# Eight of eleven gated-pair combinations built during the up rounds, and the norm work reordered at group changes

## The chip, the cores and the metric

The kernel runs on one core of a Trainium2 chip. The metric is the device time of one execution in microseconds (us), here the median of repeated runs. The engines are TensorE (PE in the profile; PEld is its weight load), VectorE (DVE), ScalarE (ACT), GpSimd (POOL) and SyncE (SP), which here only starts DMA transfers.

## What is computed

One layer of a streaming encoder on 2048 prompt and 64 sample tokens with 1024 channels. The change touches the second half of the layer, a gated feed-forward network, and the final norm:

```
h = modulate(x, norm_ffn_g, shift, scale)
up, cf_new = causal_dwconv(h @ ffn_up_w, cf_prev, ffn_conv_w, ffn_conv_b)   # 1024 -> 2 * 2816, width 3
val, gt = split(up, 2)
x = x + gate * ((val * gelu(gt)) @ ffn_down_w)                              # 2816 -> 1024
y = rmsnorm(x, final_norm_g)
```

## The kernel before

The 2112 tokens lie along the free dimension in two halves of 1056, the channels on the 128 partitions. Every matrix is held as float32 and multiplied as a pair of float16 numbers, high and low, in three passes (high by high, high by low, low by high). Large products use one level of a seven-product scheme over 2 by 2 blocks, so each operand needs seven combinations of its four blocks: some are the blocks, the others sums made of them. A combination costs the sums (GpSimd), a float16 copy of it (ScalarE, "hi") and the rest as float16 (VectorE, "lo").

**Up rounds.** 22 rounds, one for each pair of 128-row tiles (value and gate), each of 7 products times 3 token pieces `q` of 352 columns times 12 matmuls = 252 matmuls of 352 columns (`block_product`, `passes`, L2886). ScalarE copies products out of PSUM (`copy` L1658, `c21` L1666) and computes the first tap of the convolution (`first_tap` L1695) and the gelu; VectorE adds products (`block` L2547, L2550, L2553), computes two taps (`ffn_conv` L2563, L2567), multiplies value by gate (`product` L2571) and splits the next round's weights (`up_lo` L2495). SP stores the gated product of the round (the hidden tile) to DRAM as `ffn_hidden` (`store_hidden`). Beside this, 44 "units" (combinations of the down weights, `unit_*`) are made two a round, three in rounds 17 to 20, and stored to DRAM as `down_combinations`.

**Down phase.** Hidden tiles go in 11 pairs `i` (two tiles of 128 rows each). The tokens go in 3 groups `g` of 352 columns in each half, and the output rows in 4 pairs of 128-row tiles, so there are 12 steps `n = 4 g + (0..3)`; `pair_of` turns the order round in every second group, so that the weights need no reload at a group change. A step is 7 products of 11 pairs of 3 matmuls, 231 matmuls of 352 columns (`down_product`, L3131), cut into chunks of pairs (`chunks_of`) so that weights of the next step can be loaded into `dwt` as soon as a chunk is through. `dact` has 11 slots, one for each pair, with the seven combinations of one group. In every group all 11 slots are filled from `ffn_hidden`: a load into one of two staging buffers (`base_load`, L937), four sums on GpSimd (`base_sums`, L1146 to L1151), two copies on ScalarE (`base_hi`, L1727, L1729), two subtractions on VectorE (`base_lo`, L2584, L2586):

```
dve.wait_ge(b_hi, 2 * s + 1)
dve.tensor_tensor(dact[i][:, 0:3, 1], stage_of(s)[:, 1:4], dact[i][:, 0:3, 0], ALU.subtract)
dve.wait_ge(b_hi, 2 * s + 2)
dve.tensor_tensor(dact[i][:, 3:7, 1], dsum[s % 2], dact[i][:, 3:7, 0], ALU.subtract)
```

A slot may be overwritten when the last step of the group has used it, and in group 0 when the up phase's `hTc` under it is free. The queues are written out by hand, in program order for each engine. At a group change (n = 3 and 7) ScalarE and VectorE have `base_hi`/`base_lo` of five pairs ahead of the first evacuation of step n, another in the middle, and the others after it. The evacuation of a step is `first_copy` (ScalarE L1849), `fourth_copy`, and on VectorE `top_left` to `bottom_left` with the residual update `y_update` (L2679); it is followed by squares (`square2`) and their sum over tiles (`add_square`, L2731, L2733). After four steps TensorE sums over partitions by a float32 matmul with ones (`sum_squares2`, L3095), placed between products of the next group's first chunk, ScalarE takes the root (`root2`, L1868), VectorE the reciprocal (`inverse`, L2737) and the scaling (`finish`, L2740), and SP stores y (L967, `store_y`) and loads the next residual (L961).

## Time and profile before

| what | value |
|---|---|
| median of 3 runs | 2797.05 us (2796.39 to 2802.14) |
| profiled execution, its own time | 2797.01 us |
| its span in the profile | 2794.9 us |
| TensorE busy | 2674.5 us, 96% |
| VectorE, ScalarE, GpSimd busy | 1761.8, 1367.9, 580.9 us |
| up rounds | 1433.8 to 2264.0 us of the span |
| down phase, to TensorE's last matmul | 2264.0 to 2783.8 us |

The span is the profiled part of the execution; 2.1 us of its time lie outside. Busy shares are averages over stages with different limits, and PE counts as busy at half clock too.

### The profile page before, as it was taken

To read this page: it belongs to the slowest core of one execution; us is meant where nothing else is said; L and a number is where in the kernel's file an instruction comes from. 1 tells how busy PE (TensorE), PEld (TensorE's weight loads), DVE (VectorE), ACT (ScalarE), POOL (GpSimd) and SP (SyncE) were. 2 spreads that over 40 slices of the span, in tenths; PEclk is the share of its full clock that TensorE was granted. 3 is DMA by queue.
4 is the path that set the end of the run, shared out by engine and by line. 5 is a ranking of instruction groups with operands and counts; after the bars stand their busy time and mean duration, and the time that the engine had idled before them with its cause. 6 is when DMAs were issued, how large, how long until landed. Compare 5 with 4: busy or idle time off the path is not lost. (4 is left out here: it accounts for less than half of the span.)

```text
span 2794.9 us, 50241 instructions
## 1 busy us (share of the span) xinstructions
PE 2674.5 (96%) x18662; PEld 1786.5 (64%) x18662; DVE 1761.8 (63%) x3321; ACT 1367.9 (49%) x2618; POOL 580.9 (21%) x603
## 2 busy tenths in 40 slices
PE   7999999999999999999999999999999988879797
PEld 2466666666678886559986666666666655546464
DVE  4966464646466665777787766667777773462723
ACT  4966574747466662125565444544445542232311
POOL 2600000000047894000001010111101162431600
PEclk9999999999999999999999999999999999989898
DMA  8722122220554442656532222222222354464452
GB/s 275 209 89 101 63 69 99 75 102 24 163 162 114 121 185 93 223 189 162 152 93 97 98 81 101 84 101 97 102 99 101 128 210 173 144 210 153 131 216 88
DMA packets 206280, 361.76 MB, mean 129 GB/s; under 512 B 56784, under 2 KB 144848, under 8 KB 200992
## 3 DMA queue, kind: packets, MB, share of 16 engines
q1 hardware_dynamic: 196192, 348.10, 37.8%
q10 hardware_dynamic: 8848, 8.74, 0.9%
q8 instruction: 109, 1.79, 0.3%
q0 software_dynamic: 1072, 2.65, 0.3%
q14 instruction: 59, 0.48, 0.1%
HBM read 252.42 MB, written 109.64 MB: 130 GB/s over the span
## 5 line engine op out<-in xcount | busy, mean ns | idle before, releaser
L2886 PE MATMUL ps<-arena 128*128 128x352 f16 (+1 forms) x11880 | 1611.4, 297 | 4.6 <-DVE arena L2495 1.7
L2886 PEld LDWEIGHTS ps<-arena 128*128 128x128 f16 x11880 | 1101.3, 97 | 510.2 <-DVE arena L2062 2.3
L3131 PE MATMUL ps<-arena 128*128 128x352 f16 x2772 | 438.9, 322 | 43.8 <-DVE arena L2586 26.7
L3131 PEld LDWEIGHTS ps<-arena 128*128 128x128 f16 x2772 | 275.8, 100 | 207.5 <-DVE arena L2586 21.9
L1120 POOL TENSOR_TENSOR arena<-arena 128x128 f32<-128x128 f32 x44 | 22.8, 519 | 1038.9 <-DMA arena<-in_w_down 1038.9
L1658 ACT ACTIVATE arena<-ps 128x352 f32<-128x352 f32 x264 | 119.3, 463 | 201.2 <-PE ps L2886 201.2
L2495 DVE SCALAR_TENSOR_TENSOR arena<-arena 128x512 f16<-128x512 f32 x154 | 104.5, 692 | 142.0 <-ACT arena L1621 142.0
L2992 PE MATMUL ps<-arena 128*128 128x424 f16 (+1 forms) x960 | 173.6, 342 | 1.9 <-DVE arena L2374 1.3
L2978 PE MATMUL ps<-arena 128*128 128x64 f32 (+2 forms) x1200 | 152.2, 273 | 0.5 <-DVE arena L2338 0.5
L2978 PEld LDWEIGHTS ps<-arena 128*128 128x128 f32 (+2 forms) x1200 | 146.0, 194 | 3.3 <-issue 1.8
L1076 POOL CAST arena<-arena 64x512 f16<-64x512 f32 x8 | 4.9, 608 | 688.2 <-DMA arena<-in_cache_kT 688.0
L2992 PEld LDWEIGHTS ps<-arena 128*128 128x128 f16 x960 | 92.5, 97 | 82.6 <-issue 2.3
L1297 ACT ACTIVATE arena<-ps 128x352 f32<-128x352 f32 x192 | 80.8, 462 | 121.4 <-PE ps L2886 121.4
L1695 ACT ACTIVATE arena<-arena 128x2114 f32<-128x2114 f32 x44 | 94.5, 2148 | 69.9 <-DVE arena L2550 69.7
L2563 DVE SCALAR_TENSOR_TENSOR arena<-arena 128x2114 f32<-128x2114 f32 x44 | 106.4, 2417 | 34.0 <-ACT arena L1695 34.0
L1506 ACT ACTIVATE arena<-ps 128x512 f32<-128x512 f32 (+3 forms) x136 | 76.2, 561 | 104.8 <-PE ps L2965 104.7
L1104 POOL TENSOR_TENSOR arena<-arena 128x1024 f32<-128x1024 f32 (+6 forms) x147 | 119.1, 810 | 13.8 <-POOL arena L1097 3.9
L2062 DVE SCALAR_TENSOR_TENSOR arena<-arena 128x512 f16<-128x512 f32 x112 | 73.8, 686 | 64.9 <-ACT arena L1276 64.7
L2567 DVE SCALAR_TENSOR_TENSOR arena<-arena 128x2114 f32<-128x2114 f32 x44 | 107.9, 2452 | 0.4
L1499 ACT ACTIVATE arena<-arena 128x640 f32<-128x640 f32 (+5 forms) x136 | 102.7, 755 | 4.7 <-DVE arena L2317 4.5
L2687 DVE TENSOR_TENSOR arena<-ps,arena 128x352 f32<-128x352 f32 x12 | 6.3, 523 | 151.8 <-PE ps L3131 150.5
L2317 DVE CUSTOM_DVE_ANT_0 arena<-ps,arena 128x640 f32<-128x640 f32 (+5 forms) x136 | 100.2, 737 | 0.3 <-issue 0.2
(234 smaller groups left out, 3418.8 us busy)
## 6 DMA issues: line engine op xcount, KB each, us to landing
arena<-ffn_hidden SPq DMA_DIRECT2D x33, 704.0 KB, 4.1
arena<-in_w_up SPq DMA_DIRECT2D x44, 512.0 KB, 3.9
down_combinations<-arena SPq DMA_DIRECT2D x44, 448.0 KB, 2.7
arena<-down_combinations SPq DMA_DIRECT2D x10, 1792.0 KB, 7.1
arena<-down_combinations SPq DMA_DIRECT2D x20, 896.0 KB, 6.3
arena<-gates SPq DMA_DIRECT2D x8, 2112.0 KB, 9.5
arena<-in_w_proj SPq DMA_DIRECT2D x32, 512.0 KB, 4.4
gates<-arena SPq DMA_DIRECT2D x16, 1024.0 KB, 7.6
```

The lines of the kernel that those rows point to most:

```text
L1104: pool.tensor_tensor(out, djunk[:, :, 0:w], djunk[:, :, w:2 * w], ALU.add).then_inc(ada_step, 1)
L1499: act.activation(pr[0:x.rows, x.h, 0:x.w], pr[0:x.rows, x.h, 0:x.w], ACT.Exp, scale=-1.0, bias=least[0:x.rows, x.h:x.h + 1], accum_out=sm[ ...
L1658: act.activation(fcp[(0, 1, 2, 0)[i]][q], ps[:, bank_of((0, 2, 3, 4)[i], q), 0:CF], ACT.Copy, scale=CSF)\
L1695: act.activation(out, u[:, 0:LF], ACT.Identity, scale=w0, bias=fb).then_inc(f_tap, 1)
L2317: dve.tensor_tensor_reduce(pr[0:rows, h, 0:w], src, bias[x.b][0:rows, h, x.b0:x.b0 + w], 1.0, 3.0e38, ALU.add, ALU.min, least[0:rows, h:h ...
L2495: dve.scalar_tensor_tensor(fsp[:, c, :, 1, :], src.rearrange("p (k m) -> p k m", k=4), -WSF if c == 6 else WSF, fsp[:, c, :, 0, :], ALU.mu ...
L2563: dve.scalar_tensor_tensor(out, u[:, 1:1 + LF], tap(1), out, ALU.mult, ALU.add).then_inc(f_conv, 1)
L2567: dve.scalar_tensor_tensor(out, u[:, 2:2 + LF], tap(2), out, ALU.mult, ALU.add).then_inc(f_conv, 1)
L2886: mm = pe.matmul(out, wt[:, k, wp, :], act_t[:, k, hp], start=(first and k == 0 and n == 0), stop=(last and k == K - 1 and n == 2), skip_g ...
L2978: mm = pe.matmul(ps[0:x.rows, 6, 64 * x.h:64 * x.h + 64], pt[0:k, x.h, c * P:c * P + x.rows], vv[x.b][0:k, x.v0 + c, 64 * x.h:64 * x.h + 6 ...
L2992: mm = pe.matmul(out, wt[:, wp, k, :], mixT[:, k, hp, t:t + w], start=(k == k0 and m == 0), stop=(k == k1 - 1 and m == 2))
L3131: mm = pe.matmul(ps[:, down_bank(n, k), 0:CF], dwt(i)[:, wi, wp, :], dact[i][:, bi, hp, :], start=(i == 0 and m == 0), stop=(i == NI - 1 a ...
```

## The change

- Of the 11 pairs, the first 8 (`NQ`) have their combinations made during up rounds 3 to 18, as 48 "items": one item is one pair in one of six pieces of 176 columns in each half (`HW`). An item is a load of 704 columns from `ffn_hidden`, four sums of 176 columns (`four_sums`), two copies (`item_hi`), two subtractions (`item_lo`), and a store of 4928 bytes a partition to the new DRAM tensor `hidden_combinations`. There are three items and two units in each of these 16 rounds, three units in rounds 1, 2, 19 and 20. Items have one input buffer (`itemr`), one for sums (`isum`), and one for the result (`iout`).
- In the down phase the slots 0 to 7 are filled by one DMA each (`slot_load`). Pairs 8 to 10 (`NB` = 3) go on as before, now as halves of 2 by 176 columns.
- A combination that was a sum by itself now replaces a block in the buffer (`four_sums`, `unit_sums`), so that four combinations are split with the blocks and three with the sums, and `FACTORS` follows.
- The last step of a group goes in seven chunks, single pairs at first; step 10 ends in single pairs.
- At a group change the order on ScalarE and VectorE is the whole evacuation of the step, then a pair, a root or reciprocal, a pair, the other root or reciprocal, a pair. The reciprocal goes to a buffer of its own (`grs`); scaling and store of the third and fourth tile pairs move behind the evacuation of the next two steps. `sum_squares2` stands one product later.

```diff
+NB = 3
+NQ = NI - NB
+HW = CF // 2
...
+        itemr = at_(46914, 4 * HW).rearrange("p (b t) -> p b t", b=4)
+        isum = at_(47618, 3 * HW).rearrange("p (b t) -> p b t", b=3)
+        iout = at_(52000, 7 * 2 * HW, F16).rearrange("p (c s t) -> p c s t", c=7, s=2)
...
-        dact = [at_(3584 + 7 * CF * i, 7 * 2 * CF, F16).rearrange("p (c s t) -> p c s t", c=7, s=2) for i in range(NI)]
+        dact = [at_(3584 + 7 * CF * i, 7 * 2 * CF, F16).rearrange("p (w c s t) -> p w c s t", w=2, c=7, s=2) for i in range(NI)]
...
+            if n == ND - 1:
+                return [(0, NI)]
+            if n % 4 == 3:
+                return [(i, i + 1) for i in range(4)] + [(4, 6), (6, NQ), (NQ, NI)]
+            if n == ND - 2:
+                return [(0, 4), (4, NQ)] + [(i, i + 1) for i in range(NQ, NI)]
+            return [(0, 4), (4, NQ), (NQ, NI)]
...
-        FACTORS = ((0, 0), (1, 2), (4, 5), (3, 3), (5, 4), (6, 1), (2, 6))
+        FACTORS = ((1, 1), (2, 3), (5, 5), (4, 4), (0, 0), (6, 2), (3, 6))
...
+        def units_of(f):
+            return [3 * f - 3 + u for u in range(3)] if f < 3 else [3 * f - 19 + u for u in range(3)]
+        def loop_units(i, late):
+            return [4 * i + 6 + 2 * late + u for u in range(2)]
+        def loop_items(i, late):
+            return [(6 * i + 3 * late + u, (3 * late + u) // 2, (3 * late + u) % 2) for u in range(3)]
...
+            def item_load(n, i, q):
+                sp.wait_ge(b_lo, 2 * n + 2)
+                sp.wait_ge(h_stored, 192 * i + 192)
+                sp.dma_start(itemr.rearrange("p b t -> p (b t)"),
+                             hid_d[:, q, ds(2 * i, 2)].rearrange("p k h t -> p (k h t)")).then_inc(b_loaded[0], 16)
+            def item_store(n, i, q):
+                sp.wait_ge(b_lo, 2 * n + 4)
+                sp.dma_start(hdc_d[:, q // 2, ds(i, 1), q % 2].rearrange("p a c s t -> p (a c s t)"),
+                             iout.rearrange("p c s t -> p (c s t)")).then_inc(item_stored, 16)
...
+            def loop_transfers(i, late):
+                f = round_a(i) + late
+                (n0, _, _), (n1, _, _), (n2, _, _) = loop_items(i, late)
+                u0, u1 = loop_units(i, late)
+                q = 3 * late
+                up_tiles(f + 1)
+                item_store(n0, i, q)
+                item_load(n1, i, q + 1)
+                store_hidden(f - 1)
+                item_store(n1, i, q + 1)
+                item_load(n2, i, q + 2)
+                unit_store(u0)
+                unit_load(u1)
+                item_store(n2, i, q + 2)
+                if late:
+                    item_load(n2 + 1, i + 1, 0)
+                else:
+                    item_load(n2 + 1, i, 3)
+                unit_store(u1)
+                unit_load(u1 + 1)
...
+            def slot_load(g, i):
+                sp.dma_start(dact[i].rearrange("p w c s t -> p (w c s t)"),
+                             hdc_d[:, g, i].rearrange("p w c s t -> p (w c s t)")).then_inc(a_loaded[i // 4], 16)
...
+            first_slots(0, 1)
             store_hidden(LAST - 1)
-            base_load(2)
-            base_load(3)
-            base_load(4)
-            sp.wait_ge(p_filled, up_done(LAST, 3, 2))
+            first_slots(1, 3)
+            first_slots(3, 5)
             weight_load(0, 1, 0)
-            base_load(5)
+            first_slots(5, 7)
+            first_slots(7, 8)
             sp.wait_ge(p_filled, up_done(LAST, 6, 2))
             weight_load(0, 1, 1)
             sp.wait_ge(f_ev, 6 + 6 * NF)
             sp.wait_ge(f_c22, 3 * NF)
             weight_load(0, 2, 0)
             weight_load(0, 2, 1)
-            base_load(6)
-            base_load(7)
             store_hidden(LAST)
             weight_load(0, 2, 2)
+            base_load(2)
...
+                if i == 3:
+                    for k in range(NQ):
+                        sp.wait_ge(q_filled, pair_used(n, k))
+                        slot_load(g + 1, k)
+                    base_load(NB * (g + 1) + 2)
                     store_y(g, 0)
+                    continue
+                if i == 2 and g < NG - 1:
+                    base_load(NB * (g + 1))
+                    base_load(NB * (g + 1) + 1)
+                if n:
+                    next_weights(n, 0)
+                if g and i == 0:
+                    next_residual(g - 1, 0)
+                    store_y(g - 1, 1)
+                if g and i == 1:
+                    store_y(g - 1, 3)
+                next_weights(n, 1)
+                if g and i == 0:
+                    next_residual(g - 1, 1)
+                if g and i == 1:
+                    next_residual(g - 1, 3)
+                next_weights(n, 2)
+                if g and i == 0:
+                    store_y(g - 1, 2)
+                    next_residual(g - 1, 2)
...
+            def four_sums(blocks, sums, at0):
+                b12, b11, b22, b21 = blocks
+                t0, t2, t3 = sums
+                pool.tensor_tensor(t0, b12, b11, ALU.subtract).then_inc(b_sum, 1)
+                pool.wait_ge(b_sum, at0 + 1)
+                pool.tensor_tensor(b12, b22, b12, ALU.subtract).then_inc(b_sum, 1)
+                pool.tensor_tensor(t2, b22, t0, ALU.subtract).then_inc(b_sum, 1)
+                pool.wait_ge(b_sum, at0 + 3)
+                pool.tensor_tensor(t3, b21, t2, ALU.subtract).then_inc(b_sum, 1)
...
+            def loop_sums(i, late):
+                (n0, _, _), (n1, _, _), (n2, _, _) = loop_items(i, late)
+                u0, u1 = loop_units(i, late)
+                item_sums(n0)
+                item_sums(n1)
+                unit_sums(u0)
+                item_sums(n2)
+                unit_sums(u1)
...
+            def item_hi(n):
+                act.wait_ge(item_stored, ITEM_BASE + 16 * n)
+                act.wait_ge(b_sum, 4 * n + 4)
+                act.activation(iout[:, 0:4, 0], itemr, ACT.Copy).then_inc(b_hi, 1)
+                act.activation(iout[:, 4:7, 0], isum, ACT.Copy).then_inc(b_hi, 1)
...
-            def ffn_round(f, late=False):
-                units = [] if tile_is(f, LAST) else wu_units(f, late)
+            def ffn_round(f, units, items=()):
                 if not tile_is(f, 1):
                     for q in range(3):
                         c21(f - 1, q)
...
                     act.wait_ge(p_filled, up_done(f - 1, c, 2))
                     up_hi(f, c)
                 first_tap(f - 1, 1)
+                if items:
+                    item_hi(items[0][0])
                 for q in range(3):
                     copy(f, 0, q)
                 gelu(f - 1, 0)
                 gelu(f - 1, 1)
                 pads(f)
                 copy(f, 1, 0)
+                if items:
+                    item_hi(items[1][0])
...
             for n in range(ND):
-                g, last = n // 4, n % 4 == 3 and n < ND - 1
-                s = NI * (g + 1)
-                if last:
-                    for k in range(5):
-                        base_hi(s + k)
+                g, s = n // 4, NB * (n // 4 + 1)
                 first_copy(n)
-                if last:
-                    base_hi(s + 5)
                 fourth_copy(n)
                 for k in range(4):
                     square2(n, k)
                     if n == ND - 1 and k == 2:
                         root2(g, 0)
-                if last:
-                    base_hi(s + 6)
-                    base_hi(s + 7)
-                    for h in range(2):
-                        root2(g, h)
-                    for k in range(8, NI):
-                        base_hi(s + k)
+                if n % 4 == 3 and n < ND - 1:
+                    base_hi(s)
+                    root2(g, 0)
+                    base_hi(s + 1)
+                    root2(g, 1)
+                    base_hi(s + 2)
             root2(NG - 1, 1)
...
+            def item_lo(n):
+                dve.wait_ge(b_hi, 2 * n + 1)
+                dve.tensor_tensor(iout[:, 0:4, 1], itemr, iout[:, 0:4, 0], ALU.subtract).then_inc(b_lo, 1)
+                dve.wait_ge(b_hi, 2 * n + 2)
+                dve.tensor_tensor(iout[:, 4:7, 1], isum, iout[:, 4:7, 0], ALU.subtract).then_inc(b_lo, 1)
...
-            def ffn_round(f, late=False):
+            def ffn_round(f, units, items=()):
                 ffn_conv(f - 1, 0)
+                if items:
+                    item_lo(items[0][0])
                 up_lo(f, 5)
                 up_lo(f, 6)
...
+                if items:
+                    item_lo(items[1][0])
...
+                    if items and q == 0:
+                        item_lo(items[2][0])
...
+                    if n >= 4:
+                        dve.wait_ge(norm_rs, 2 * NE + 2 * (n // 4 - 1) + h + 1)
...
-                    base_lo(s + 6)
-                    base_lo(s + 7)
-                    for h in range(2):
-                        inverse(g, h)
-                    for k in range(4):
-                        finish(g, k)
-                        if k < 3:
-                            base_lo(s + 8 + k)
+                    base_lo(s)
+                    inverse(g, 0)
+                    base_lo(s + 1)
+                    inverse(g, 1)
+                    finish(g, 0)
+                    base_lo(s + 2)
+                    finish(g, 1)
+                if g and n % 4 < 2:
+                    finish(g - 1, n % 4 + 2)
...
+                        if n % 4 == 0 and i in (0, 4):
+                            pe.wait_ge(a_loaded[i // 4], A_BASE + 64 * g + 64)
+                        if n % 4 == 0 and i >= NQ:
+                            pe.wait_ge(b_lo, LO_BASE + 2 * (NB * g + i - NQ + 1))
...
-                        if n in (4, 8) and x == 0 and k in (1, 3):
-                            sum_squares2(n // 4 - 1, k // 2)
+                        if n in (4, 8) and x == 0 and k in (2, 4):
+                            sum_squares2(n // 4 - 1, k // 2 - 1)
```

The order of instructions on VectorE in an up round: L2649 and L2653 of the change (L2563 and L2567 before) are `ffn_conv`, L2581 (L2495) is `up_lo`, L2669 and L2671 are `item_lo`. Before, from the value's convolution to the gate's:

```order
L2563 SCALAR_TENSOR_TENSOR arena<-arena 128x2114
L2564 COPY arena<-arena 128x2
L2565 COPY arena<-arena 128x2
L2567 SCALAR_TENSOR_TENSOR arena<-arena 128x2114
L2495 SCALAR_TENSOR_TENSOR arena<-arena 128x4x128 x2
L2563 SCALAR_TENSOR_TENSOR arena<-arena 128x2114
```

The same place in a round of the change with items, where rows of address arithmetic (ISA, REGISTER_ALU) show too:

```order
L2653 SCALAR_TENSOR_TENSOR arena<-arena 128x2114
L2668 ISA
L2669 TENSOR_TENSOR arena<-arena 128x4x176
L2670 REGISTER_ALU
L2671 TENSOR_TENSOR arena<-arena 128x3x176
L2580 REGISTER_ALU
L2581 SCALAR_TENSOR_TENSOR arena<-arena 128x4x128
L2580 REGISTER_ALU
L2581 SCALAR_TENSOR_TENSOR arena<-arena 128x4x128
L2648 REGISTER_ALU
L2649 ISA
L2649 SCALAR_TENSOR_TENSOR arena<-arena 128x2114
```

The item's two subtractions stand between the value's convolution and the weight splits; two more items stand further on, behind `product` and between the evacuations of the third piece.

VectorE at the first group change, step 3: before, the end of the five pairs, the first evacuation (L2687, L2679), the sixth pair, and the second evacuation:

```order
L2584 TENSOR_TENSOR arena<-arena 128x3x352
L2586 TENSOR_TENSOR arena<-arena 128x4x352
L2687 TENSOR_TENSOR arena<-ps,arena 128x352
L2679 SCALAR_TENSOR_TENSOR arena<-arena 128x352
L2584 TENSOR_TENSOR arena<-arena 128x3x352
L2586 TENSOR_TENSOR arena<-arena 128x4x352
L2695 TENSOR_TENSOR arena<-ps,arena 128x352
L2733 TENSOR_TENSOR arena<-arena 128x352
```

The change, from the last evacuation of step 3 (L2813, L2773) and its squares (L2829) on; L2676 and L2678 are `base_lo`, L2833 `inverse`, L2836 `finish`, L2781 the first evacuation of step 4:

```order
L2813 TENSOR_TENSOR arena<-ps,arena 128x352
L2773 SCALAR_TENSOR_TENSOR arena<-arena 128x352
L2829 TENSOR_TENSOR arena<-arena 128x352 x2
L2676 TENSOR_TENSOR arena<-arena 128x2x4x176
L2678 TENSOR_TENSOR arena<-arena 128x2x3x176
L2833 RECIPROCAL arena<-arena 128x352
L2676 TENSOR_TENSOR arena<-arena 128x2x4x176
L2678 TENSOR_TENSOR arena<-arena 128x2x3x176
L2833 RECIPROCAL arena<-arena 128x352
L2836 TENSOR_TENSOR arena<-arena 128x2x352 x2
L2676 TENSOR_TENSOR arena<-arena 128x2x4x176
L2678 TENSOR_TENSOR arena<-arena 128x2x3x176
```

Nothing of the next group stands ahead of the evacuation any more, and three pairs stand where eleven stood.

SP at the same place, before, from step 3 into step 4 (L937 `base_load`, L967 `store_y`, L961 residual, L943, L946 and L950 the three lots of weights):

```order
L937 DMA arena<-ffn_hidden 128x1408 x11
L967 DMA out_y<-arena 256x1x352 x2
L943 DMA arena<-down_combinations 128x7168
L967 DMA out_y<-arena 256x1x352 x2
L961 DMA arena<-x_after_mixers 128x2x352 x2
```

And the change, from behind the slot loads of step 3 to the second lot of weights in step 5 (L1027 `store_y`, L1021 residual, L1003, L1006 and L1010 the lots):

```order
L1027 DMA out_y<-arena 256x1x352 x2
L1003 DMA arena<-down_combinations 128x7168
L1021 DMA arena<-x_after_mixers 128x2x352 x2
L1027 DMA out_y<-arena 256x1x352 x2
L1006 DMA arena<-down_combinations 128x3584 x2
L1021 DMA arena<-x_after_mixers 128x2x352 x2
L1010 DMA arena<-down_combinations 128x1792 x3
L1027 DMA out_y<-arena 256x1x352 x2
L1021 DMA arena<-x_after_mixers 128x2x352 x2
L1003 DMA arena<-down_combinations 128x7168
L1027 DMA out_y<-arena 256x1x352 x2
L1006 DMA arena<-down_combinations 128x3584 x2
```

The stores of y that followed each other now stand between the lots of weights of two steps, the fourth ahead of the second lot of step 5.

## Rows read from the trace of the kernel before

**Rows 1.** The page: engines' busy time, and granted clock in 40 slices.
```profile
PE 2674.5 (96%) x18662; PEld 1786.5 (64%) x18662; DVE 1761.8 (63%) x3321; ACT 1367.9 (49%) x2618; POOL 580.9 (21%) x603
...
PEclk9999999999999999999999999999999999989898
```
**Rows 2.** TensorE's waits by releaser: total us, times, longest us.
```profile
PE ps L3095 <- DVE arena L2733: 31.9, 3, 14.9
PE ps L3131 <- DVE arena L2586: 26.7, 8, 7.7
PE ps L3131 <- ACT arena L1849: 10.5, 2, 5.7
...
PE ps L3131 <- ACT arena L1666: 4.2, 1, 4.2
...
PE ps L3131 <- DMA arena<-down_combinations: 2.3, 1, 2.3
```
**Rows 3.** Timeline, TensorE in the down phase: start, length, what, [idle before].
```profile
2264.03 7.36 PE L3131 MATMUL ps<-arena 128*128 128x352 f16 x48
...
2324.15 108.53 PE L3131 MATMUL ps<-arena 128*128 128x352 f16 x723 [2.02 <-DVE arena L2586]
...
2456.95 1.54 PE L3095 MATMUL ps<-arena 128*128 128x352 f32 x2 [14.87 <-DVE arena L2733]
...
2463.76 0.75 PE L3095 MATMUL ps<-arena 128*128 128x352 f32 x2
...
2745.01 27.93 PE L3131 MATMUL ps<-arena 128*128 128x352 f16 x174 [2.34 <-DMA arena<-down_combinations]
...
2782.59 1.21 PE L3095 MATMUL ps<-arena 128*128 128x352 f32 x2 [4.11 <-DVE arena L2733]
```
**Rows 4.** Windows by stage: busy us (x instructions) by engine, clock, DMA share, GB/s.
```profile
2327.00:2432.00 105.00, 105.00 (x703) 68.05 (x701) 35.82 (x51) 24.71 (x37) 21.27 (x18) 1.00 0.46 165
2432.00:2466.00 34.00, 13.73 (x60) 7.13 (x59) 27.73 (x26) 16.43 (x21) 22.39 (x18) 0.70 0.33 103
```
**Rows 5.** The same for one up round with two units, one with three.
```profile
2036.00:2073.80 37.80, 37.80 (x255) 24.52 (x254) 26.08 (x36) 18.81 (x34) 3.87 (x8) 1.00 0.27 97
...
2150.00:2188.00 38.00, 38.00 (x257) 24.62 (x256) 27.83 (x39) 19.77 (x36) 6.23 (x12) 1.00 0.32 113
```
**Rows 6.** Timeline, ScalarE at the border of two up rounds.
```profile
1846.21 2.15 ACT L1695 ACTIVATE arena<-arena 128x2114 f32<-128x2114 f32 x1 [4.23 <-DVE arena L2550]
1848.27 0.44 ACT L1666 ACTIVATE arena<-ps 128x352 f32<-128x352 f32 x1
...
1850.74 0.44 ACT L1669 ACTIVATE arena<-ps 128x320 f32<-128x320 f32 x1 [1.33 <-PE ps L2886]
```
**Rows 7.** Timeline, VectorE: convolution, product, base_lo, add_square.
```profile
2263.23 1.62 DVE L2586 TENSOR_TENSOR arena<-arena 128x1408 f16<-128x1408 f32 x1
2264.77 2.41 DVE L2563 SCALAR_TENSOR_TENSOR arena<-arena 128x2114 f32<-128x2114 f32 x1
...
2288.37 3.08 DVE L2571 SCALAR_TENSOR_TENSOR arena<-arena 128x2114 f32<-128x2114 f32 x1
...
2398.97 1.17 DVE L2733 TENSOR_TENSOR arena<-arena 128x352 f32<-128x352 f32 x2
```
**Rows 8.** Timeline, ScalarE: the larger copy of base_hi.
```profile
2254.82 1.37 ACT L1729 ACTIVATE arena<-arena 128x1408 f16<-128x1408 f32 x1
```
**Rows 9.** Timeline, GpSimd: a unit's sum, two sums of a pair.
```profile
1822.87 0.46 POOL L1120 TENSOR_TENSOR arena<-arena 128x128 f32<-128x128 f32 x1 [23.81 <-DMA arena<-in_w_down]
...
2237.85 0.93 POOL L1151 TENSOR_TENSOR arena<-arena 128x352 f32<-128x352 f32 x1
2238.74 3.05 POOL L1146 TENSOR_TENSOR arena<-arena 128x352 f32<-128x352 f32 x1
```
**Rows 10.** DMA issues: count, KB each, median us to landing.
```profile
arena<-ffn_hidden SPq DMA_DIRECT2D x33, 704.0 KB, 4.1
...
arena<-down_combinations SPq DMA_DIRECT2D x20, 896.0 KB, 6.3
```

271 lines of the change are left out of this document (123 added, 148 removed).

## Prediction

> **What bounds the kernel now.** I read the page first: TensorE is busy 96% of the span and its granted clock is full but for the last fifth [rows 1]. So time can only come out of TensorE's stream, and only where it waits or runs at half clock. Its waits by releaser show where: 31.9 us in front of the float32 sums (L3095) on `add_square`, 26.7 us in front of the down products on `base_lo`, 10.5 us on `first_copy`, 4.2 us on `c21`, 2.3 us on weights [rows 2]. All of these lie behind 2264 us. There the timeline shows three holes: the start of group 0, where products begin at 2264.03 and run freely only from 2324.15; the group change near 2440, where one float32 sum waits 14.87 us; and the same again one group later [rows 3]. The windows by stage separate what is bound by what: in 2327 to 2432 TensorE does 703 matmuls in 105 us at full clock while VectorE is busy for 36; in 2432 to 2466 it does 60 in 34 us at clock 0.70 while VectorE is busy for 28 [rows 4]. At the holes the chain GpSimd sums, ScalarE copy, VectorE subtraction sets the time: eleven pairs a group, of which some stand ahead of the evacuation in both queues. In an up round TensorE is never idle, and VectorE is busy for 26.1 of 37.8 us, ScalarE for 18.8, GpSimd for 3.9 [rows 5]: this is the room into which the work moves.
>
> **The stretch of the down phase, if nothing waited.** The rate is 105/703 = 0.1494 us a matmul [rows 4]. 12 steps of 231 make 2772 matmuls, 414.1 us; six pairs of float32 sums at 0.75 us add 4.5 [rows 3]. Sum 418.6 us. Now it takes from 2264.0 to 2783.8 (2782.59 + 1.21) [rows 3], 519.8 us. So 101.2 us are lost, 75.6 of them as waits ([rows 2] for the terms above: 31.9 + 26.7 + 10.5 + 4.2 + 2.3), the rest at half clock behind them: the first sum after the 14.87 us wait took 1.54 us for what takes 0.75 shortly after [rows 3].
>
> **Start of group 0.** Before, step 0 ends about 2327.3 (21 matmuls behind 2324.15 [rows 3]), 63.3 us after the start; bare it is 34.5. The change has slots 0 to 7 loaded by DMA, 1.26 MB each. No row shows such a load; the nearest is two of 0.9 MB issued together, 1.8 MB landed after 6.3 us [rows 10], by which one slot takes 4.4 us or less. The loads start between 27 and 5 us before the round's end, as `hTc` comes free; TensorE wants slots 0 to 3 at its end and 4 to 7 12.6 us later (84 matmuls). At 4.4 us each they are in time. The 4.2 us wait on `c21` goes, since ScalarE has no `base_hi` ahead of it. What is late next is pair 10, whose hidden tile is the last product. Up end E; first tap of the gate E + 0.7 to E + 2.9 (2.15 us [rows 6]); two taps of 2.4 us [rows 7] to E + 7.8; two gelus, about 2.1 us by the length of the first tap, to E + 9.9; product 2.4 to 3.1 us [rows 7] to E + 12.5; six store issues and their landing, about 5.5 us as a 0.7 MB DMA takes 4.1 [rows 10], to E + 18; load 4.1 us to E + 22; four sums of 0.93 us [rows 9] to E + 26; two copies, 1.37 us for 1408 columns [rows 8] and 1.0 for 1056, to E + 28.5; the last subtraction to E + 30. It is needed at E + 31.4 (210 matmuls). So no wait, with 1.4 us to spare. Gain 63.3 - 34.5 = 28.8 us.
>
> **Group changes.** The evacuation of a step ends about 3.8 us after its last matmul: the last two additions of squares of step 2 run from 2398.97 to 2400.14 [rows 7], and its last matmul ends at 2396.3 by the count of 21 + 462 matmuls from 2324.15 [rows 3]. The change puts the float32 sum behind three products of the next first chunk, 36 matmuls or 5.4 us. So it waits for nothing. The second sum needs the root of the first: sum 0.75, `base_hi` 2.4 and root 0.6 leave it ready near 8 us, it is asked for at 9.7. Slots 0 to 7 are loaded as single pairs of step 3 finish, 3.1 us apart. The three pairs left: VectorE has pair 8 by 7, pair 9 by 13 and pair 10, whose load waits for pair 8, by about 21 us (reciprocals 2.4 each, pairs 3 each, scaling 1.7); TensorE wants pair 10 at 27 us. So both changes should go through bare. Left of the 101.2 us are then only the end (4.1 us of wait, 0.5 of half clock [rows 3]) and what follows.
>
> **Weights.** Ahead of step 6's second lot SP now waits for the fourth store of y, which waits for `finish` behind step 5's evacuation: 3.8 + 1.7 = 5.5 us into step 6. The lot is wanted at 12.6 us; store issues 1.2 us, landing 6.3 us [rows 10] plus the store's bytes, gives 13 to 15. I take 1 us of wait, twice (steps 6 and 10). The 2.3 us at step 11 becomes about 0.5, since its last lot is cut into single pairs and only the last comes late. Cost 2.5 us in all.
>
> So the down phase loses 4.6 + 2.5 = 7.1 in place of 101.2 us: gain 94.1.
>
> **Up rounds.** Each of 16 rounds gets three items. An item has 704 + 528 = 1232 columns on VectorE, 1232/1408 of 1.62 = 1.42 us [rows 7]; on ScalarE 1232/1408 of 1.37 = 1.2 us [rows 8]; on GpSimd four sums of 176 columns, between 0.46 (128) and 0.93 (352) [rows 9], I take 0.56. A round: VectorE 26.1 + 4.3 = 30.4, ScalarE 18.8 + 3.6 = 22.4, GpSimd 3.9 + 6.7 = 10.6 us of 37.6. Nobody is full, so the price is nothing unless order or contention makes a wait. Two places. First, `item_lo` behind the value's convolution stands in front of the gate's, and its `item_hi` comes only behind the gate's first tap: VectorE waits some 1.6 us, and with 1.4 of work everything behind is 3 us later; the waits for weights further on take that up. Second, the third item stands in front of the last evacuations, and these release the first tap, which stands in front of `c21`, which frees the bank for TensorE's next round. `c21` ends at 1848.71 and TensorE wants it at 1850.74, where the next round begins [rows 6]: 2.0 us of room, less 1.4, leaves 0.6. In time, unless that item comes late: it hangs on a chain product, six stores, a store, a load, sums, copy.
>
> GpSimd and VectorE disturb each other: a sum that takes 0.93 us alone took 3.05 while VectorE was in a long two-input instruction, and the product took 3.08 where a convolution tap of the same size takes 2.41 [rows 7, 9]. If each of the twelve sums of a round held VectorE up by its own length, VectorE would get 6.7 us more a round, 37.1 of 37.6, and with its 1.6 us of waiting 38.7. I take the likelier case that most fall into its pauses, and 0.25 us a round: 4 us. Ends: nothing, and 1.5 us a round, 24 us.
>
> The Trainium skill (SBUF — State Buffer, Who interferes with whom) says that a VectorE instruction with two SBUF inputs and a GpSimd instruction that reads SBUF exclude each other for their whole length. By that rule, the trace agrees, and it speaks against twelve more sums a round: by it the worst case of the last paragraph, 18 us in place of 4, would be the sum's, if all of them fall on such work.
>
> TensorE's operand now comes as two runs of 176 columns. No row here shows that form; the nearest is the same width in one run, so I take the same 0.1494. An extra 1% would be 4 us; fewer columns move nothing, so no gain.
>
> **Sum.** The profiled execution took 2797.01 us, span 2794.9 and 2.1 outside; the median, 2797.05, is the same. Less 94.1, plus 4 for the up rounds, plus 1 for the first group change's exposed pieces: 2708 us.
>
> **Rivals.**
>
> 1. *VectorE becomes the bound of the up rounds.* The third item comes late and with it `c21`. For: 30.4 us of work and at least 1.6 us of waiting, 0.6 us of room, contention shown. Against: long pauses behind the weight splits, and TensorE never waited for anyone in these rounds. At 1.1 us a round (38.7 in place of 37.6) it costs 18 us in place of 4: 2722, up to 2740 at 2.2 us. It decides once the third item is more than 0.6 us later than I have it.
> 2. *The holes stay in part.* Pair 10 has only 1.4 us to spare at the start; at a group change the roots wait behind `base_hi`. A wait of 5 to 8 us at each of the three places, with half clock behind it as now, is 20 to 25 us: 2725 to 2733. For: each chain crosses four engines and DMA. Against: three pairs where eleven stood, and 6 us of room at the changes.
> 3. *Slower.* The up rounds lose more than the down phase gains: the point is 94/16 = 5.9 us a round. It needs VectorE at 43.5 us a round, such as when every item's load, stores and sums run one after another with ScalarE standing at `item_hi` each time. At 7 us a round: 2797 - 94 + 112 = 2815.
> 4. *It does not do what it says*: slot loads are too slow at a group change and bring the old wait back. The loads have 44 us from the first freed slot to the use of slot 4, and two of 0.9 MB in 6.3 us [rows 10] make 35 us for all eight. At double that, 26 us of wait come back at both changes: 2760.
>
> **How the numbers follow.** Forecast, 2698 to 2716: 0.56. Rival 1, 2716 to 2745: 0.24. Rival 2, 2716 to 2740: 0.15. Rival 3: 0.03. Rival 4: 0.02. The prediction is 2708. The low end is no loss in the up rounds and none at the weights (2797 - 96.6 = 2700, less 2 for clock); the high end takes in most of rivals 1 and 2: 2698 to 2738. A measurement of this kernel tells 0.2% (5.6 us) from no change; faster 0.96, same 0.01, slower 0.03.
>
> **What would show it.** Right: TensorE's stream from the end of the up rounds to its end in 426 us; waits on `base_lo` and in front of the first two pairs of float32 sums near nothing; the last round ends within 5 us of 2264; clock full in all slices but the last. Wrong at the weights: a wait on `down_combinations` at steps 6 and 10 of none or of more than 3 us. Wrong in the up rounds: rounds of 38.5 us or more, with waits on `c21` (ScalarE) once a round. What would break the prediction is a late third item in every round, or a slot load that lands behind the first use.

## The result, and the profile after

| | before | after |
|---|---|---|
| median | 2796.72 us (2791.28 to 2802.14, 4 runs) | 2768.97 us (2766.91 to 2769.89, 4 runs) |
| ratio, 95% interval | | 0.990 (0.988 to 0.992) |
| span of the profiled execution | 2794.9 us | 2766.1 us |
| up rounds end at | 2264.0 us | 2327.9 us |
| from there to TensorE's last matmul | 519.8 us | 427.0 us |

The change is 28 us faster. Forecast were 89 us, 2708 (2698 to 2738), and 2769 lies outside the range. The last two rows split the miss: the down phase became 92.8 us shorter, forecast 94.1; but it starts 63.9 us later, forecast 4.

The down phase first: TensorE's timeline of the kernel after, in the same stretches as [rows 3] (start, duration, form, count, idle time and its releaser).

```profile
2327.94 31.50 PE L3225 MATMUL ps<-arena 128*128 128x352 f16 x210
2359.66 5.54 PE L3225 MATMUL ps<-arena 128*128 128x352 f16 x36 [0.22 <-DVE arena L2678]
...
2471.60 0.75 PE L3187 MATMUL ps<-arena 128*128 128x352 f32 x2
...
2550.59 24.65 PE L3225 MATMUL ps<-arena 128*128 128x352 f16 x164 [1.54 <-DMA arena<-down_combinations]
...
2692.09 48.22 PE L3225 MATMUL ps<-arena 128*128 128x352 f16 x322 [2.25 <-DMA arena<-down_combinations]
...
2753.39 1.54 PE L3187 MATMUL ps<-arena 128*128 128x352 f32 x2 [4.14 <-DVE arena L2829]
```

The first 210 matmuls of group 0 run without a pause, where [rows 3] had a hole from 2264 to 2324 us; the wait ahead of the last pair (L2678 is `base_lo`) is 0.22 us. The float32 sums at the group changes take 0.75 us a pair and wait for nothing, where one had waited 14.87. Two waits for weights are left, 1.54 and 2.25 us, and the one at the end.

Now the place where the time went: the waits by releaser of the kernel after, on TensorE over the whole span.

```profile
PE ps L2978 <- ACT arena L1757: 43.3, 17, 3.5
...
PE ps L3187 <- DVE arena L2829: 4.1, 1, 4.1
PE ps L3225 <- DMA arena<-down_combinations: 3.8, 2, 2.2
```

L1757 is `c21`, L2978 the up products. Before, `c21` cost 4.2 us once, at the start of the down phase, and nothing in the up rounds; now it costs 43.3 us in 17 waits. The first, 2.2 us, stands ahead of the rounds with items, and every kernel below has one like it; the other 16, 41.1 us, are one for each round with items. The timeline shows two rounds of them:

```profile
1965.44 40.42 PE L2978 MATMUL ps<-arena 128*128 128x352 f16 x252 [3.47 <-ACT arena L1757]
2007.05 25.23 PE L2978 MATMUL ps<-arena 128*128 128x352 f16 x168 [1.20 <-ACT arena L1757]
2032.58 12.70 PE L2978 MATMUL ps<-arena 128*128 128x352 f16 x84 [0.29 <-ACT arena L1749]
2048.75 6.47 PE L2978 MATMUL ps<-arena 128*128 128x352 f16 x31 [3.47 <-ACT arena L1757]
```

From 1965.44 to 2048.75 are two rounds in 83.31 us, 41.66 each. A round had been 37.6 (252 matmuls at the 0.1494 of the prediction), so 4.06 us are lost, times 16 rounds 65 us. Of the 4.06, 2.7 are waiting (41.1 us for `c21` and 2.4 for `copy`, L1749, over 16); the rest is mostly half clock behind the longer waits: the 252 matmuls behind the first one of 3.47 us took 40.42, and in their first 4 us only 14 ran, at a granted clock of 0.50 (here and below, a row of windows ends in the granted clock, the DMA share and GB/s):

```profile
1965.50:1969.50 4.00, 4.00 (x14) 2.03 (x15) 4.00 (x4) 3.73 (x6) 3.86 (x3) 0.50 0.32 100
```

Is an engine full? The windows by stage over those two rounds (busy time of each engine, granted clock, DMA share, GB/s), against [rows 5]:

```profile
1965.40:2048.80 83.40, 78.41 (x505) 49.49 (x506) 63.64 (x85) 42.93 (x79) 33.22 (x41) 0.97 0.47 158
```

None is. VectorE works 31.8 us of a 41.7 us round, ScalarE 21.5, GpSimd 16.6, the DMA engines 0.47 of the time. So somebody waits in turn. The waits by releaser of the other engines, 1507 to 2215 us:

```profile
POOL arena L1202 <- DMA arena<-ffn_hidden: 388.0, 48, 13.2
ACT arena L1808 <- POOL arena L1207: 139.5, 48, 4.5
...
DVE arena L2669 <- ACT arena L1808: 71.6, 32, 3.5
```

L1202 and L1207 are the first and the last sum of an item, L1808 is `item_hi`, L2669 `item_lo`. GpSimd stands at the load of all 48 items, ScalarE at the sums of all 48, VectorE at the copies of 32. Each of these steps finds its engine standing at it. The chain of waits, followed back from the end over most of a round, shows why that adds up (start, duration, what):

```profile
2013.01 0.80 ACT arena L1808
...
2015.26 1.29 DVE arena L2581 x2
2016.55 2.33 DVE arena L2649
...
2019.04 2.43 DVE arena L2653
...
2022.49 1.08 ACT arena L1792
2023.59 2.37 DVE arena L2657
...
2029.30 2.15 DMA ffn_hidden<-arena
2031.61 3.67 DMA arena<-ffn_hidden
...
2036.35 0.88 POOL arena L1204
...
2039.56 0.63 ACT arena L1809
2040.19 0.35 ACT arena L1749
2040.54 0.53 ACT arena L1711
...
2042.93 0.71 DVE arena L2671
2043.80 0.33 SPq L941
2044.53 3.58 DMA arena<-ffn_hidden
```

First comes the copy of the round's first item (L1808), and its subtractions stand in VectorE's queue ahead of two weight splits (L2581) and the gate's two taps (L2649, L2653). Then the gelu (L1792), the product (L2657), the six stores of the hidden tile (L917 to L921), and the third item: load, sums, copies, subtraction (L2671), the issue of its store (L941) and, behind that, the load of the next item. There is no matmul in it. Behind the last subtractions stand VectorE's last evacuations (L2636), the first tap (ScalarE, 2046.19 to 2048.34) and `c21`, for which TensorE waits.

The second item runs beside the taps and the product, and it arrives just as late: SyncE's timeline has the sixth store issued by 2030.0 us, and the last subtraction of the second item ends at 2030.8, so its store, issued at 2030.95, and the load behind it wait for the item in truth. So the items make a chain of their own. `itemr`, `isum` and `iout` exist once, and SyncE issues the load of item n+1 behind the store of item n, which waits for its last subtraction. The 48 items are one closed chain, and a round cannot be shorter than three trips around it. From load to load the trips are, in this round, 2002.76 to 2018.54, to 2031.61, to 2044.53. By the timelines of the engines they are made of (us):

| item | load, to the first sum | four sums | copies and subtractions | to the issue of the next load | trip |
|---|---|---|---|---|---|
| first | 3.9 | 6.3 | 2.4 | 3.2 | 15.8 |
| second | 6.9 | 2.7 | 2.6 | 0.8 | 13.1 |
| third | 3.8 | 3.4 | 4.8 | 0.9 | 12.9 |
| all | 14.6 | 12.5 | 9.8 | 4.9 | 41.8 |

That the trips add up to the round proves nothing, since load to load a round later is a round whatever holds it. What counts is that they leave no gap: GpSimd starts as the load lands, ScalarE and VectorE start as the step before ends or behind a few short pieces of their own, and SyncE stands at the subtractions. The 3.2 us of the first item are the two weight splits behind its subtractions, for which the up tiles' transfers wait, and the issue of these ahead of the item's store.

### The profile page after: what moved, and what is told of

Read it like the earlier page. It is cut to its first block, busy times and chain, and to the rows that moved or that the text cites. A ratio compares the mean times of both kernels' runs of the same rounds, so it can differ in the third digit from the quotient of the medians.

```text
span 2766.1 us, 50644 instructions
## 1 busy us (share of the span) xinstructions
PE 2669.9 (97%) x18662; PEld 1778.4 (64%) x18662; DVE 1747.0 (63%) x3369; ACT 1355.8 (49%) x2666; POOL 639.6 (23%) x699
## 3 DMA queue, kind: packets, MB, share of 16 engines
q0 software_dynamic: 1072, 2.65, 0.3%
## 4 chain that ended last, share of the span: by engine, by line
PE 57%; DVE 11%; DMA 10%; POOL 7%; ACT 7%; issue 5%; SPq 2%; DVEq 1%; ACTq 0%; POOLq 0%
PE ps L2978 32%; PE ps L3225 13%; DMA arena<-ffn_hidden 5%; PE ps L3070 4%; PE ps L3057 3%; PE ps L3046 2%; POOL arena L1204 2%; POOL arena L1207 2%; DVE arena L2653 2%; DVE arena L2649 2%; DMA arena<-in_w_mod_rest 2%; DVE arena L2657 1%; DMA ffn_hidden<-arena 1%; PE ps L2902 1%; PE ps L3084 1%
## 5 line engine op out<-in xcount | busy, mean ns | idle before, releaser
L2978 PE MATMUL ps<-arena 128*128 128x352 f16 (+1 forms) x11880 | 1633.7, 299 | 50.4 <-ACT arena L1757 43.3
L2978 PEld LDWEIGHTS ps<-arena 128*128 128x128 f16 x11880 | 1105.2, 97 | 574.4 <-ACT arena L1757 49.4
L3225 PE MATMUL ps<-arena 128*128 128x352 f16 x2772 | 415.2, 310 | 4.0 <-DMA arena<-down_combinations 3.8
L1202 POOL TENSOR_TENSOR arena<-arena 128x176 f32<-128x176 f32 (+1 forms) x57 | 49.2, 863 | 688.7 <-DMA arena<-ffn_hidden 688.7
L2581 DVE SCALAR_TENSOR_TENSOR arena<-arena 128x512 f16<-128x512 f32 x154 | 112.8, 771 | 64.1 <-ACT arena L1711 64.1
L1192 POOL TENSOR_TENSOR arena<-arena 128x128 f32<-128x128 f32 x44 | 23.1, 526 | 506.0 <-DMA arena<-in_w_down 506.0
L2781 DVE TENSOR_TENSOR arena<-ps,arena 128x352 f32<-128x352 f32 x12 | 6.3, 525 | 210.4 <-PE ps L3225 179.7
L1749 ACT ACTIVATE arena<-ps 128x352 f32<-128x352 f32 x264 | 115.2, 459 | 35.1 <-PE ps L2978 35.1
L2649 DVE SCALAR_TENSOR_TENSOR arena<-arena 128x2114 f32<-128x2114 f32 x44 | 108.6, 2467 | 34.4 <-ACT arena L1786 34.4
L2148 DVE SCALAR_TENSOR_TENSOR arena<-arena 128x512 f16<-128x512 f32 x112 | 73.9, 687 | 64.8 <-ACT arena L1366 64.6
L2653 DVE SCALAR_TENSOR_TENSOR arena<-arena 128x2114 f32<-128x2114 f32 x44 | 111.2, 2528 | 0.2
```

Of the source, the lines that this page charges most:

```text
L1749: act.activation(fcp[(0, 1, 2, 0)[i]][q], ps[:, bank_of((0, 2, 3, 4)[i], q), 0:CF], ACT.Copy, scale=CSF)\
L2581: dve.scalar_tensor_tensor(fsp[:, c, :, 1, :], src.rearrange("p (k m) -> p k m", k=4), -WSF if c == 6 else WSF, fsp[:, c, :, 0, :], ALU.mu ...
L2649: dve.scalar_tensor_tensor(out, u[:, 1:1 + LF], tap(1), out, ALU.mult, ALU.add).then_inc(f_conv, 1)
L2653: dve.scalar_tensor_tensor(out, u[:, 2:2 + LF], tap(2), out, ALU.mult, ALU.add).then_inc(f_conv, 1)
L2978: mm = pe.matmul(out, wt[:, k, wp, :], act_t[:, k, hp], start=(first and k == 0 and n == 0), stop=(last and k == K - 1 and n == 2), skip_g ...
L3225: mm = pe.matmul(ps[:, down_bank(n, k), 0:CF].rearrange("p (w t) -> p w t", w=2), dwt(i)[:, wi, wp, :], dact[i][:, :, bi, hp, :], start=(i ...
```

## The experiments

All but the first are orders of the same work, or the same order with one piece of work taken out or added; all are made on the kernel after. "Ring" is the theory above, the closed chain of the items. The rival is that of the prediction, VectorE's work as the bound, and with it that the sums beside VectorE are what costs. Rounds are read from TensorE's timeline, as the mean of 15 rounds between waits on `c21`, or where there are none from the 840 matmuls in 125.46 us that stand in one piece.

| label | median us (lowest to highest) | ratio to before, 95% | a round, us | waits on `c21`, us |
|---|---|---|---|---|
| (after) | 2768.97 (2766.91 to 2769.89) | 0.990 (0.988 to 0.992) | 41.66 | 43.3, 17 times |
| no_items | 2705.75 (2702.01 to 2709.29) | 0.9685 (0.9661 to 0.9709) | | 2.0, once |
| first_ahead | 2743.9 (2742.13 to 2748.84) | 0.983 (0.9804 to 0.9855) | 40.2 | 32.5, 17 times |
| second_ahead | 2784.06 (2779.93 to 2790.88) | 0.9971 (0.9957 to 0.9984) | 42.6 | 62.8, 17 times |
| both_ahead | 2739.55 (2733.87 to 2745.09) | 0.9813 (0.9789 to 0.9836) | 39.9 | 26.8, 17 times |
| load_before_store | 2730.53 (2729.93 to 2731.7) | 0.9776 (0.9757 to 0.9794) | 39.0 | 22.2, 16 times |
| new_order | 2701.93 (2697.55 to 2713.01) | 0.9668 (0.9651 to 0.9685) | 37.6 | 2.1, once |
| no_sums | 2707.07 (2705.71 to 2708.66) | 0.9694 (0.9675 to 0.9713) | 37.6 | 1.9, once |
| more_vector | 2779.87 (2774.09 to 2788.18) | 0.9955 (0.9939 to 0.997) | 42.3 | 57.4, 17 times |

The first four ran beside a before of 2794.76 us (15 runs), the last four beside one of 2794.14 (15 runs).

**no_items.** What does the down phase give by itself? The 48 items are left out, and the slots 0 to 7 are loaded from the weights' combinations, so the down products are made from other numbers, but from as many bytes.

```diff
-                item_store(n0, i, q)
-                item_load(n1, i, q + 1)
...
-                             hdc_d[:, g, i].rearrange("p w c s t -> p (w c s t)")).then_inc(a_loaded[i // 4], 16)
+                             wdc_d.rearrange("p n c s m -> p (n c s m)")[:, 4928 * i:4928 * i + 4928]).then_inc(a_loaded[i // 4], 16)
```

> The 48 items are left out altogether (no loads, sums, copies, subtractions or stores for them in the up rounds), and the slots 0 to 7 are filled in the down phase by loads of the same size from the tensor of down combinations, so the output is not the reference's; everything behind the up rounds is as in the change. Both theories: the up rounds return to 37.6 us each, TensorE has no wait on c21 in them, the down phase stays at 427 us, and the whole is the prediction without its allowance for the up rounds, 2700 to 2706 us. If the up rounds stay above 38 us, the loss there is not the items' but that of the finer hidden stores or of the loop written out twice.

2705.75 us. The down products begin at 2268.73 us, where they began at 2264.03 before and at 2327.94 after. From the first wait on `c21`, the one ahead of the rounds with items, it is 751.8 us to there and was 816.9 after: 65 us, or 4.07 for each of 16 rounds. So the loss of the change lies in the items, and the slot loads are not too slow. This run doesn't tell the theories apart; it only sets the floor.

**first_ahead.** One link of the ring is shortened: the store of the first item and the load of the second go ahead of the 1 MB of up tiles.

```diff
-                up_tiles(f + 1)
                 item_store(n0, i, q)
                 item_load(n1, i, q + 1)
+                up_tiles(f + 1)
                 store_hidden(f - 1)
```

> SP's order in a round with items: store of item 0 and load of item 1 ahead of the two up weight tiles, nothing else. Ring theory (the items share one buffer, so that load, sums, copies, subtractions and the next load form one closed chain of 41.7 us a round, and that chain sets the round): the load of item 1 is issued 2.4 us earlier and lands about 3 us sooner after its issue, but the load of item 2 still stands behind the six hidden stores, whose issue ends 0.8 us before the item's store is issued now. So only 0.8 to 0.9 us a round come out, 16 rounds, 14 us: 2755 us. VectorE theory (its added 4.3 us of work and its collisions with GpSimd set the round): no change, 2769 within 5 us, as its work is the same.

2743.9 us: 25 us off, where 14 were expected. No engine has less work, and the round is 1.5 us shorter. The direction is the ring's; the size of the link was taken too small.

**second_ahead.** The same at the second place: store of the second item and load of the third ahead of the six stores of the hidden tile.

```diff
                 item_load(n1, i, q + 1)
-                store_hidden(f - 1)
                 item_store(n1, i, q + 1)
                 item_load(n2, i, q + 2)
+                store_hidden(f - 1)
                 unit_store(u0)
                 unit_load(u1)
```

> SP's order in a round with items: store of item 1 and load of item 2 ahead of the six hidden stores, nothing else. Ring theory: item 1 is finished 0.8 us after the last hidden store is issued now, so nothing is won by going ahead of them: within 5 us of 2769, perhaps some us less because the load no longer shares the DMA engines with the hidden tile, or some more because the hidden tile is stored later. VectorE theory: no change either. This run is the control for the pair.

2784.06 us: 15 us slower than the kernel after, a miss of the expectation. The waits by releaser, 1507 to 2215 us, show what I had overlooked:

```profile
POOL arena L1202 <- DMA arena<-ffn_hidden: 351.4, 48, 13.1
...
ACT arena L1802 <- POOL arena L1197: 76.2, 33, 4.8
...
POOL arena L1192 <- DMA arena<-in_w_down: 60.7, 18, 16.5
```

The items wait less for their loads (351.4 for 388.0). But the issue of the six stores, which ran while the second item was being made, now stands between the third item's load and the unit's transfers. In one round of SyncE's timeline the unit's next load is issued 6.2 us behind the third item's (1952.21 to 1958.43) where it had been 3.8 (2031.61 to 2035.43), and GpSimd stands 60.7 us at that load in 18 waits (L1192) where it had been 27.7 in 3. The unit's sums then run from 1961.72 to 1964.79, beside VectorE's steps for the third item: the split, the addition and the two subtractions in front of the item's store take 0.89, 0.78, 1.14 and 0.95 us where they took 0.69, 0.52, 0.89 and 0.70. With that the third trip takes 14.0 us in place of 12.9, and the first two are what they were. L1802 is `unit_hi`, which waited 31.3 us for its sums (L1197) in the kernel after and 76.2 here; but it is done when the first tap begins, which waits for VectorE's evacuation, and new_order below has 73.8 us of this wait with no wait of TensorE behind it. So it is a sign that the unit is late, not what holds the round.

**both_ahead.** Both edits.

> Both orders together. Ring theory: item 1 is ready when the product ends, its subtractions end 1.9 us behind it, and the load of item 2 goes out about 2.9 us earlier than now, its landing 0 to 1 us shorter: a round of 38 to 39 us in place of 41.7, 2711 to 2730 us, most likely 2722. It is more than the sum of the two single edits, which the ring theory alone expects. VectorE theory: no change, 2769 within 5 us.

2739.55 us, 29 us off where the two single edits give 10 together (25 off and 15 on), as only the ring expects; but 4 us less than first_ahead and 10 above the expected range. `item_hi` waited 62.1 us for its sums in 1507 to 2215 us where it had been 139.5: both links are shorter. Two things are left in the round from 1900.53 to 1940.48. The second item's subtractions stand behind the product in VectorE's queue, and begin at 1923.54 though its copies ended at 1922.98. And the third trip is 14.1 us (1926.42 to 1940.48), as in second_ahead, with the unit's sums again beside its subtractions (1.14 and 0.96 us). So an order has to serve the items and the units. That these two make up all the 1 to 2 us missing was not tested.

**load_before_store.** The other link: the load of item n+1 overwrites only `itemr`, which the first of the two subtractions of item n reads. It waits for that one, and is issued ahead of the store of item n.

```diff
             def item_load(n, i, q):
-                sp.wait_ge(b_lo, 2 * n + 2)
+                sp.wait_ge(b_lo, 2 * n + 1)
...
                 up_tiles(f + 1)
-                item_store(n0, i, q)
                 item_load(n1, i, q + 1)
+                item_store(n0, i, q)
                 store_hidden(f - 1)
```

(and likewise at the second and third item)

> On the changed kernel; the load of the next item waits only for the first of the two subtractions of the item before (the second reads the sums, not what the load overwrites) and is issued ahead of that item's store instead of behind it. Nothing else is moved. Ring theory (each item's load, sums, copies, subtractions and store follow one another through single buffers, and their sum is the round): the second subtraction (0.7 us) and the issue of the store (0.6 us) leave the chain three times, 3.5 to 4 us off a round of 41.7: 2705 to 2720. VectorE theory (VectorE's work is the round): no work goes, so 2769 within 4.

2730.53 us, 38 us off, of 49 to 64 expected. A round is 39.0 us, so 2.6 of the 3.5 to 4 us came. Same bytes, same engine work, two semaphore values and three places in a queue: VectorE as the bound is out as the whole explanation. What still holds the round? The chain of waits has this in one round of it:

```profile
1914.37 6.09 DMA arena<-ffn_hidden
...
1920.63 2.17 POOL arena L1202
...
1926.29 0.92 DVE arena L2671
...
1930.61 0.84 DVE arena L2664
1931.60 2.76 DMA down_combinations<-arena
1934.51 0.63 ACT arena L1809
```

The second item's load still stands behind the up tiles and takes 6.1 us, and its first sum falls on the product and takes 2.2. Further on the view leads through the unit's subtraction (L2664) and the landing of its store to L1809; but L1809, the second copy of the item, waits in the program for no store of a unit and follows L1808 without a pause, and the next `unit_hi`, at 1937.88, waited for its own sums. So that the units hold this round is not shown.

**more_vector.** If VectorE were the bound, more work there would cost its full length. Four splits of 128x512 are put ahead of the split of combination 3. VectorE stood idle 3.3 us a round one split later, ahead of that of combination 4, so the splits of 3 and 4 move into the hole.

```diff
                 for c in range(5):
+                    if items and c == 3:
+                        dve.wait_ge(p_hi, 7 * NR + 7 * (f + 1) + c + 1)
+                        for k in range(4):
+                            dve.scalar_tensor_tensor(fsp[:, c, :, 1, :], fsum[:, 0].rearrange("p (k m) -> p k m", k=4),
+                                                     WSF, fsp[:, c, :, 0, :], ALU.mult, ALU.subtract).then_inc(e_sum, 1)
+                            dve.wait_ge(e_sum, 4 * NE + 4 * f - 11 + k)
                     up_lo(f + 1, c)
```

> On the changed kernel; VectorE does four more splits of 128x512 (0.69 us each, 2.8 us with their waits) in each of the 16 rounds with items, at the place where it stands idle for 3.3 us, ahead of the split of combination 3. Their results are overwritten by that split. Ring theory: the round is the chain of the items and VectorE has room there: 2769, within 5. VectorE theory: 2.8 us more a round, 2814.

VectorE's timeline of one round of it:

```profile
1951.89 2.25 DVE L2581 SCALAR_TENSOR_TENSOR arena<-arena 128x512 f16<-128x512 f32 x3
1954.07 3.83 DVE L2741 SCALAR_TENSOR_TENSOR arena<-arena 128x512 f16<-128x512 f32 x4
1957.93 1.69 DVE L2581 SCALAR_TENSOR_TENSOR arena<-arena 128x512 f16<-128x512 f32 x2
```

The four took 3.83 us, more than the 2.8 that I had counted, and the round grew by 0.7, to 42.3: the median is 11 us above after, where 45 were forecast by VectorE's theory and, at 3.83 us, 61 would be. The idle time swallowed 3.1 of 3.8 us. It is 6 us beyond the ring's range: the extra work is longer than the hole, by 0.5 us a round, an estimated 8 us.

**no_sums.** The item sums are left out, everything else stays.

```diff
-        isum = at_(47618, 3 * HW).rearrange("p (b t) -> p b t", b=3)
+        isum = itemr[:, 1:4]
...
                 pool.wait_ge(b_lo, 2 * n + 2)
-                four_sums([itemr[:, k] for k in range(4)], [isum[:, k] for k in range(3)], 4 * n)
+                pool.sem_inc(b_sum, 4)
```

> On the changed kernel; GpSimd leaves out the four sums of each of the 48 items and only reports them done; the three combinations that are sums are made from the item's second to fourth block instead, with the same copies and subtractions, so the output is not the reference's. Loads, stores, ScalarE's and VectorE's work stay. Ring theory: 12.6 us (6.4 + 2.8 + 3.4) leave the chain of a round of 41.7, and TensorE is the bound again: 2703 to 2715. If the transfers behind the up tiles set the round and the sums run in their shadow: above 2750. If VectorE's own work is the bound, only what the sums held it up goes: 2750 to 2769.

2707.07 us, rounds of 37.6, TensorE without a wait. VectorE's work is all there and is done in time, so it is not the bound, and the transfers behind the up tiles are not either. The sums are 12.5 of the 41.8 us of the three trips, the loads 14.6; without the sums the ring is an estimated 29 us, well under TensorE's round. The run takes away both the sums' place in the chain and their disturbance of VectorE, and doesn't tell these apart; new_order does. How long they are is seen in GpSimd's timeline of the kernel after, the sums of one round's first and third item:

```profile
2006.63 0.56 POOL L1202 TENSOR_TENSOR arena<-arena 128x176 f32<-128x176 f32 x1 [7.61 <-DMA arena<-ffn_hidden]
2007.27 2.56 POOL L1204 TENSOR_TENSOR arena<-arena 128x176 f32<-128x176 f32 x1
2009.79 0.56 POOL L1205 TENSOR_TENSOR arena<-arena 128x176 f32<-128x176 f32 x1
2010.42 2.56 POOL L1207 TENSOR_TENSOR arena<-arena 128x176 f32<-128x176 f32 x1
...
2036.35 0.88 POOL L1204 TENSOR_TENSOR arena<-arena 128x176 f32<-128x176 f32 x1
```

and VectorE beside it:

```profile
2006.81 2.59 DVE L2649 SCALAR_TENSOR_TENSOR arena<-arena 128x2114 f32<-128x2114 f32 x1 [1.51 <-ACT arena L1786]
...
2009.83 2.73 DVE L2653 SCALAR_TENSOR_TENSOR arena<-arena 128x2114 f32<-128x2114 f32 x1
```

The first item's four sums take 6.3 us (2006.63 to 2012.98, the end of the fourth) for the 2.2 of four times 0.56: the second and the fourth begin while a tap is under way and take 2.56. The first and the third began before the taps and kept their 0.56.

**new_order.** If it is the order, an order that serves items and units should give the whole gain. SyncE's queue in a round becomes:

```diff
+                item_load(n1, i, q + 1)
+                item_store(n0, i, q)
                 up_tiles(f + 1)
-                item_store(n0, i, q)
-                item_load(n1, i, q + 1)
-                store_hidden(f - 1)
-                item_store(n1, i, q + 1)
                 item_load(n2, i, q + 2)
+                item_store(n1, i, q + 1)
+                store_hidden(f - 1, (0,))
                 unit_store(u0)
                 unit_load(u1)
-                item_store(n2, i, q + 2)
+                store_hidden(f - 1, (1,))
...
+                item_store(n2, i, q + 2)
```

with `item_load` waiting for the first subtraction, and `store_hidden` taking the halves to store.

> On the changed kernel; the order in SyncE's queue is written anew: load of the second item, store of the first, the up tiles, load of the third, store of the second, half of the hidden tile's stores, the unit's store and the next unit's load, the other half, load of the next round's item, store of the third; loads wait for the first subtraction only. It joins what both_ahead and load_before_store do, and keeps the unit's load early, which both_ahead gave up. Ring theory: items and units both get under TensorE's 37.7 us a round: 38.3 a round, 2715, range 2705 to 2728. If instead the work of VectorE or the length of the item sums beside it holds the round, not the order, it ends at both_ahead's 39.9 a round, 2740.

2701.93 us, 3 us under the expected range and the lowest median here (no_items and no_sums, with work left out, lie within 5 us): 3.3% below before and 2.4% below the change as it was made, with the same work in it. TensorE's timeline in the stretch of those rounds is one row:

```profile
1859.77 125.46 PE L2979 MATMUL ps<-arena 128*128 128x352 f16 x840
```

and the windows of two of its rounds:

```profile
1895.20:1970.40 75.20, 75.20 (x506) 48.64 (x505) 65.85 (x85) 43.44 (x80) 37.95 (x41) 1.00 0.53 174
```

VectorE is busy 32.9 us of a 37.6 us round, more than in the two rounds of the kernel after (31.8 of 41.7), and TensorE doesn't wait for it. The sums are no shorter (GpSimd is busy 19.0 us a round, 16.6 in the kernel after). So neither VectorE's work nor the length of the sums by itself holds the round. (The profiled execution, 2713.0 us, was the slowest of the six; the 8 us by which its item rounds begin later than in the kernel after, 1519.2 for 1511.0, lie ahead of them.) Which share is due to the earlier start of the load, behind the first subtraction, and which to the places in the queue was not separated; neither both_ahead nor load_before_store alone got there.

## Why the prediction was wrong, point by point

- **Start of group 0** (forecast: no wait, gain 28.8 us): right. Step 0 ends 34.9 us after the start, 34.5 forecast; pair 10 was 0.2 us late where 1.4 us of room had been counted.
- **Group changes** (bare): right; the five pairs of float32 sums ahead of the last took 0.75 us each, without a wait.
- **Weights** (1 us at step 6, 1 at step 10, 0.5 at step 11): place right, size 1.5, 2.25 and 0: 3.8 us in place of 2.5. **End**: 4.1 and 0.8 us, 4.6 forecast. The whole phase: 427.0 us against 425.7.
- **Operand in two runs of 176 columns**: right, 0.15 us a matmul (210 in 31.50 us).
- **Up rounds**: here it fell. The step is "Nobody is full, so the price is nothing unless order or contention makes a wait. Two places", and then 0.25 us a round, at most 1.5. Measured 4.06. The room was counted for each engine, and the lateness of one item at a time, each against the work beside it. It was never asked how long one item takes from load to next load, three times over, though the prediction had every piece: it even wrote the chain of the third item down ("a chain product, six stores, a store, a load, sums, copy") and then counted it as in time. By its own figures a trip is a load of 4.1 us, sums of 2.2, copies of 1.2, subtractions of 1.4 and, by the trace, some 0.7 for the issue of the store ahead of the next load, 9.6 us; three are 29, which fits under 37.6. The trips measured 41.8 (the table above). The sums took 12.5 for 6.7, half of it at the first item behind two taps (6.3 for 2.2). The loads took 14.6 for 12.3, and the excess is the second item's, behind the up tiles (6.9, 2018.54 to 2025.43). The rest is the places in four queues at which an item waits its turn: copies and subtractions 9.8 for 7.8, the way to the next load 4.9 for 2.1. Nine us of slack on a chain with no second buffer went that way, and 4 more.
- **GpSimd and VectorE** (worst case: VectorE held up by every sum's length, 6.7 us a round): who pays was wrong. VectorE is busy 32.9 us a round with the sums (new_order) and 31.4 without (no_sums, 62.88 us in two rounds), so it pays 1.5 us; GpSimd is busy 19.0 with and 5.5 without, 13.5 us for sums that I took at 6.7: it pays 6.8. And these stand in the ring. The Trainium skill (SBUF — State Buffer, Who interferes with whom) says that the pair of ports the two share is an exclusive lock, and that the order of issue decides who is blocked. By that rule, the trace agrees: the tap had begun at 2006.81, the sum stood from 2007.27 to 2009.83, 2.56 us, and the tap's length grew by 0.2; the third sum, begun at 2009.79, ahead of the second tap at 2009.83, took its 0.56, and that tap grew by 0.3.
- **Rival 1** (c21 late once a round, 1.1 to 2.2 us) named the symptom rightly, and the way it reaches `c21`, through a late third item. The cause it gave was wrong: VectorE's work was not the bound (more_vector, no_sums, new_order), though its taps and product stand in the chain. **Rival 3** described what happened, "when every item's load, stores and sums run one after another", but priced it only from the point where it would turn the sign, 5.9 us a round, and gave it 0.03. The same mechanism at 4 us a round stood in no case. **Rivals 2 and 4** didn't occur (waits of 0.2 us; no wait for a slot); the 20 to 25 us of rival 2 on 2708 are 2728 to 2733, not 2725.
- The 0.96 for faster was right in sign, with two thirds of the forecast gain missing. What "would show it wrong", rounds of 38.5 us or more with a wait on `c21` a round, is what the trace showed.

## What to carry to other kernels

When work is moved into the idle time of several engines through one set of buffers, busy shares don't price it: add up one trip around the buffer (load, each engine's step, its place in each queue, store, issue of the next load) with contended durations, times the trips a period, and compare it with the period. Uncontended, the trips left a quarter of the period here, and that was not enough. Look first at what the next load really has to wait for, and at what is queued between it and that; this order, with a load that waits for one subtraction instead of two, was worth 67 us here, at no work. And ask what a moved transfer now stands in front of: moving six stores behind the items put them between the items and the unit's transfers, the unit's sums then fell on VectorE's steps of the third item, and the kernel was 15 us slower.

## What the runs showed of the chip

- A GpSimd sum of 128x176 with a two-input VectorE instruction of 128x2114 already under way lasted 2.56 us for 0.56, 4.6 times as long, and that VectorE instruction 2.59 to 2.73 for 2.42. It goes the other way too, in smaller pieces: with the unit's sums beside them VectorE's subtractions of 704 and 528 columns took 1.14 and 0.95 us for 0.89 and 0.70 (second_ahead). Over a round the twelve sums cost GpSimd 13.5 us for their 6.7.
- Short waits of TensorE cost no more than their length, longer ones sometimes did. Behind each wait on `c21` of 0.29 to 1.54 us (both_ahead, first_ahead, load_before_store) the 252 matmuls of the round took 37.76 or 37.77 us. Behind waits of 1.95 to 3.5 us it went either way: 39.44 behind 1.97 and 2.30, 40.42 behind 3.47, but 37.76 behind 2.65, and behind one of 3.47 (1590.17, kernel after) the granted clock was full. Behind all of 4.2 us and more (second_ahead, more_vector) it was 39.3 to 40.0. TensorE's timeline of both_ahead with two waits of 2.13 us that went one each way, one of first_ahead, and the windows of the 4 us behind the two of both_ahead:

```profile
1904.81 37.76 PE L2978 MATMUL ps<-arena 128*128 128x352 f16 x252 [2.13 <-ACT arena L1757]
1944.71 39.44 PE L2978 MATMUL ps<-arena 128*128 128x352 f16 x252 [2.13 <-ACT arena L1757]
```

```profile
1589.06 37.76 PE L2978 MATMUL ps<-arena 128*128 128x352 f16 x252 [2.65 <-ACT arena L1757]
```

```profile
1904.80:1908.80 4.00, 3.99 (x27) 2.62 (x28) 4.00 (x4) 3.80 (x6) 3.84 (x4) 1.00 0.35 104
1944.70:1948.70 4.00, 3.99 (x16) 2.18 (x17) 4.00 (x4) 3.79 (x6) 3.84 (x4) 0.57 0.35 104
```

  Full speed, 2.4 GHz, in the first; nearly all at 1.2 GHz in the second, with 16 matmuls in place of 27.

- A load of 0.35 MB, issued behind a store of 0.6 MB, landed 3.7 us after its issue; with 1 MB of up tiles issued ahead of the two it was 6.9 us.
